# A two-layer DiT kernel on one core: the 1/rms of the q and k norm groups as a power on GpSimd, a copy moved to ScalarE, and the exponential's table loaded at another place

## The reference, cut to what matters

```python
def rmsnorm(x, g):
    xf = x.astype(jnp.float32)
    y = xf * lax.rsqrt(jnp.mean(xf * xf, axis=-1, keepdims=True) + EPS)
    return (y * g.astype(jnp.float32)).astype(x.dtype)
...
    q = (rmsnorm(q_lat, qc_g) @ w_q_up).reshape(b, n, MLA_HEADS, QK_DIM)
    kv = (rmsnorm(kv_lat, kvc_g) @ w_kv_up).reshape(b, n, MLA_HEADS, NOPE_DIM + V_DIM)
    q_nope = rmsnorm(q[..., :NOPE_DIM], qn_g)
    q_rope = rmsnorm(q[..., NOPE_DIM:], qr_g)
    k_nope = rmsnorm(kv[..., :NOPE_DIM], kn_g)
    ...
    q_rope = apply_axial_rope(q_rope, cos[:, None, :], sin[:, None, :])
    k_rope = apply_axial_rope(k_rope, cos, sin)
```

## Time and profile before

| | |
|---|---|
| median of three runs | 1451.29 us (1451.26 to 1451.75) |
| the profiled execution's own time | 1451.35 us |
| span in its trace | 1449.6 us |
| PE busy | 1416.5 us, 98% of the span |
| DVE busy | 996.3 us, 69% |
| ACT busy | 521.2 us, 36% |
| POOL busy | 86.7 us, 6% |
| mean granted TensorE clock | 0.995 of full |

### The profile page before, as it was taken

One profiled execution on the slowest core, in us unless ns is written; L12 is line 12 of the kernel. 1 busy time (PEld: TensorE's weight loads), 2 busy tenths in 40 slices (PEclk: granted clock), 3 DMA queues, 4 the chain that ended last, 5 costly groups with the idle time before them and its releaser, 6 DMA issues.

```text
span 1449.6 us, 20646 instructions
## 1 busy us (share of the span) xinstructions
PE 1416.5 (98%) x7940; PEld 1224.0 (84%) x7940; DVE 996.3 (69%) x1532; ACT 521.2 (36%) x841; POOL 86.7 (6%) x125
## 2 busy tenths in 40 slices
PE   6999899999999999999999999989999999999998
PEld 3788798889888888888888888878999888888887
DVE  5587887779866666666575678788667555555555
ACT  4352865243231122122221225476445323223322
POOL 0023700000000000000000000350000000000000
PEclk9999999999999999999999999999999999999999
DMA  9742012423543333324333412301032223322324
GB/s 389 296 131 88 1 45 73 146 88 119 184 146 117 94 122 117 121 81 158 116 100 102 144 45 64 111 15 56 4 103 91 98 90 100 99 87 89 112 91 142
DMA packets 42968, 158.62 MB, mean 109 GB/s; under 512 B 5152, under 2 KB 6560, under 8 KB 41760
## 3 DMA queue, kind: packets, MB, share of 16 engines
q1 hardware_dynamic: 42912, 157.87, 32.7%
HBM read 155.76 MB, written 2.10 MB: 109 GB/s over the span
## 4 chain that ended last, share of the span: by engine, by line
PE 84%; DVE 9%; ACT 3%; DMA 2%; issue 2%; SPq 0%; DVEq 0%; ACTq 0%
PE ps L734 68%; PE ps L653 4%; PE ps L655 4%; PE ps L654 4%; DVE w_lo L1428 1%; DMA ada_step<-in_w_step 1%; DVE tmp L1553 1%; DVE H_lo L1562 1%; PE ps L882 1%; PE ps L667 1%; DVE ss L1495 1%; DVE nmax L1771 1%; DMA w_raw<-in_w_main 1%; DVE pt_lo L1568 1%; ACT w_hi L1072 1%
## 5 line engine op out<-in xcount | busy, mean ns | idle before, releaser
L734 PE MATMUL ps<-H_hi,w_hi 128*128 128x512 f32 (+1 forms) x1280 | 448.8, 351 | 3.9 <-DVE H_lo L1562 2.6
L734 PE MATMUL ps<-H_lo,w_hi 128*128 128x512 f32 (+1 forms) x1280 | 447.4, 350 | 0.0
L734 PE MATMUL ps<-H_hi,w_lo 128*128 128x512 f32 (+1 forms) x1280 | 447.1, 349 | 0.0
L1072 ACT ACTIVATE w_hi<-w_raw 128x1024 fp32r<-128x1024 f32 x180 | 187.5, 1055 | 421.8 <-PE ps L734 368.8
L734 PEld LDWEIGHTS ps<-H_hi,w_hi 128*128 128x128 f32 x1280 | 242.3, 189 | 37.4 <-DVE H_lo L1562 3.8
L734 PEld LDWEIGHTS ps<-H_hi,w_lo 128*128 128x128 f32 x1280 | 242.2, 189 | 31.6
L734 PEld LDWEIGHTS ps<-H_lo,w_hi 128*128 128x128 f32 x1280 | 242.3, 189 | 30.8
L1575 DVE SCALAR_TENSOR_TENSOR X<-ps,mod,X 128x512 f32<-128x512 f32 (+1 forms) x296 | 181.1, 645 | 110.4 <-PE ps L734 88.1
L1428 DVE TENSOR_TENSOR w_lo<-w_raw,w_hi 128x1024 fp32r<-128x1024 f32 x180 | 221.7, 1242 | 37.3 <-ACT w_hi L1072 36.3
L734 PE MATMUL ps<-inner_hi,w_hi 128*128 128x512 f32 (+1 forms) x528 | 188.1, 356 | 0.3 <-DVE X L1575 0.3
L734 PE MATMUL ps<-inner_lo,w_hi 128*128 128x512 f32 (+1 forms) x528 | 187.5, 355 | 0.0
(11 more groups left out here) (210 smaller groups left out, 1836.7 us busy)
## 6 DMA issues: line engine op xcount, KB each, us to landing
w_raw<-in_w_main SPq DMA_DIRECT2D x182, 512.0 KB, 3.3
ada_raw<-in_w_ada SPq DMA_DIRECT2D x73, 512.0 KB, 4.1
ada_step<-in_w_step SPq DMA_DIRECT2D x7, 2048.0 KB, 16.7
X<-in_x SPq DMA_DIRECT2D x2, 1024.0 KB, 6.5
cb<-in_cvec SPq DMA_DIRECT2D x2, 1024.0 KB, 7.2
out_x<-X SPq DMA_DIRECT2D x8, 256.0 KB, 4.0
rtab<-in_rope SPq DMA_DIRECT2D x4, 384.0 KB, 9.2
X<-in_ctx SPq DMA_DIRECT2D x1, 1024.0 KB, 19.5
```

Of the source, the lines that this page charges most:

```text
L734: ins = pe.matmul(job.ps(a, b), ww[:, wsl], xx[:, xk, a:b], start=first and n == 0, stop=last and n == 2)
L1072: act.activation(w_hi[c % 4][:], w_raw[c % 2][:], ACT.Copy).then_inc(chunk_hi, 1)
```

## The change

It has five parts.

1. The root and the reciprocal of the 12 sums become one power with the exponent -0.5, on POOL: `inverse_root_q` (8 columns, both groups of q) and `inverse_root_k` (4 columns). ACT's `root_part` and DVE's `inverse` are gone. The mean's division is folded into the tables and gains (a factor of the root of 64 or 128).
2. DVE adds width times epsilon to the sums ahead of the power (`with_eps`), once for q and once for k.
3. Of the powers, those of tile 0 stand inside the rotation of the rotary key, and those of tile t+1 behind the addition of tile t, each in POOL's one stream.
4. The rounded copy of the rotated part goes from POOL to ACT (`rotated_hi`): that of tile t-1 stands between the square of k and the copy of v of tile t; in layer 0 that of tile 5 stands ahead of `turned_hi(5)`.
5. The one-column exponential goes from line 1334 to right behind the root of the latents, where from then on no root follows before the attention.

```diff
         pool.memset(lat_ss[:], 1.0).then_inc(consts, 1)
+        pool.memset(part_eps[:, 0:4], ROPE * EPS)
+        pool.memset(part_eps[:, 4:12], NOPE * EPS)
+        pool.memset(part_pow[:], -0.5)
...
-        def rotate(src, n, tab, done, before, scratch):
+        def rotate(src, n, tab, done, before, scratch, root_q, root_k):
...
             pool.tensor_tensor(a, src, rtab[:, tab, 0:n], ALU.mult).then_inc(done, 1)
+            root_q(0)
             for h in range(2):
...
             last.then_inc(done, 1)
+            root_k(0)
             pool.wait_ge(done, before + 2)
             pool.tensor_tensor(src, a, b, ALU.add).then_inc(done, 1)
...
+            def inverse_root_q(t):
+                pool.wait_ge(b_rt[L], parts(L, t, "q"))
+                pool.tensor_tensor(part_rms[:, t % 2, 0:8], part_sums[:, t % 2, 0:8], part_pow[:, 0:8], ALU.pow).then_inc(b_rc[L], 1)
+
+            def inverse_root_k(t):
+                pool.wait_ge(b_rt[L], parts(L, t, "k"))
+                pool.tensor_tensor(part_rms[:, t % 2, 8:12], part_sums[:, t % 2, 8:12], part_pow[:, 8:12], ALU.pow).then_inc(b_rc[L], 1)
...
                 pool.tensor_tensor(src, rgain[:], rope_b[:], ALU.add).then_inc(b_rot[L], 1)
-                pool.wait_ge(b_rot[L], 5 * t + 3)
+                if t + 1 < qtok(L):
+                    inverse_root_q(t + 1)
+                if t + 1 < TOK:
+                    inverse_root_k(t + 1)
+                pool.wait_ge(b_rot[L], 5 * t + 4)
                 hi, lo = (q_rs[L][t % 2][:, :, ROPE * n:ROPE * (n + 1)] for n in range(2))
-                pool.tensor_copy(hi.bitcast(F32R), src).then_inc(b_rot[L], 1)
-                pool.wait_ge(b_rot[L], 5 * t + 4)
                 pool.tensor_tensor(lo, src, hi, ALU.subtract).then_inc(b_rot[L], 1)
+            for t in range(qtok(L) + 1, TOK):
+                inverse_root_k(t)
...
             act.activation(lat_ss[:], lat_ss[:], ACT.Sqrt).then_inc(lat_rt[L], 1)
+            act.activation(warm[:, 0:1], ones[:, 0:1], ACT.Exp)
...
+            def rotated_hi(t):
+
+                act.wait_ge(b_rot[L], 5 * t + 3)
+                src = qn[t % 2][:, 0:ROPES].rearrange("p (h f) -> p h f", h=HEADS)
+                act.activation(q_rs[L][t % 2][:, :, 0:ROPE].bitcast(F32R), src, ACT.Copy).then_inc(b_rot[L], 1)
...
-                if t < qtok(L):
-                    root_part(t, "rope")
-                    root_part(t, "nope")
+                if 0 < t <= qtok(L):
+                    rotated_hi(t - 1)
...
-                root_part(t, "k")
...
-            act.activation(warm[:, 0:1], ones[:, 0:1], ACT.Exp)
+            if qtok(L) == TOK:
+                rotated_hi(TOK - 1)
             turned_hi(TOK - 1)
...
-            dve.tensor_scalar(qg[:, 0:1], V(L, V_QN), SCALE, None, ALU.mult).then_inc(tab_ok[L], 1)
+            dve.tensor_scalar(qg[:, 1:2], V(L, V_KN), NOPE ** 0.5, None, ALU.mult)
+            dve.tensor_scalar(qg[:, 0:1], V(L, V_QN), SCALE * NOPE ** 0.5, None, ALU.mult).then_inc(tab_ok[L], 1)
...
+            def with_eps(t, first, last):
+
+                cols = slice(4 * KINDS.index(first), 4 * KINDS.index(last) + 4)
+                dve.wait_ge(b_sum[L], sections(L, t, last))
+                dve.tensor_tensor(part_sums[:, t % 2, cols], part_sums[:, t % 2, cols], part_eps[:, cols],
+                                  ALU.add).then_inc(b_rt[L], 1)
...
                     sums(t, "nope", q_sq[L][:, ROPES:HEADS * HQ], NOPE)
+                    with_eps(t, "rope", "nope")
                 dve.wait_ge(b_sq[L], parts(L, t, "k"))
                 sums(t, "k", kn[m][:], NOPE)
+                with_eps(t, "k", "k")
                 if t < qtok(L):
-                    inverse(t, "rope", "nope")
+                    dve.wait_ge(b_rc[L], parts(L, t, "q"))
...
-                dve.wait_ge(b_sum[L], sections(L, t, "k"))
-                inverse(t, "k", "k")
+                dve.wait_ge(b_rc[L], parts(L, t, "k"))
```

More of the change, by code:

```diff
@@ L179, in build @@
     part_rms = sb("part_rms", [P, 2, 12])
+    part_eps = sb("part_eps", [P, 12])
+    part_pow = sb("part_pow", [P, 12])
     tok_rms = sb("tok_rms", [P, 8])
@@ L1267, in turned_hi @@
                 job.ready(act)
-                for kind, dst, o, scale in (("q", q, 0, qg[:, 0:1]), ("k", k, 512, V(L, V_KN))):
+                for kind, dst, o, scale in (("q", q, 0, qg[:, 0:1]), ("k", k, 512, qg[:, 1:2])):
                     if kind == "k" or t < qtok(L):
@@ L1645, in _ @@
                 gb = rgain[:, n:n + 1].to_broadcast([P, TOK, ROPE])
[L1646 removed]
+                dve.scalar_tensor_tensor(rtab[:, n], rtab[:, n], SCALE * ROPE ** 0.5 if n < 2 else 1.0, gb, ALU.mult,
                                          ALU.mult).then_inc(tab_ok[L], 1)
[L1648 removed]
+            dve.tensor_scalar(qg[:, 1:2], V(L, V_KN), NOPE ** 0.5, None, ALU.mult)
+            dve.tensor_scalar(qg[:, 0:1], V(L, V_QN), SCALE * NOPE ** 0.5, None, ALU.mult).then_inc(tab_ok[L], 1)
             ada = 0
@@ L1721, in sums @@
                                   ALU.add).then_inc(b_sum[L], 1)
-            def inverse(t, first, last):
-                x = part_rms[:, t % 2, 4 * KINDS.index(first):4 * KINDS.index(last) + 4]
-                dve.wait_ge(b_rt[L], sections(L, t, last))
-                dve.reciprocal(x, x).then_inc(b_rc[L], 1)
-                dve.wait_ge(b_rc[L], parts(L, t, "k" if last == "k" else "q"))
+            def with_eps(t, first, last):
[3 more added lines that the diff above has]
+                                  ALU.add).then_inc(b_rt[L], 1)
             def normed(t):
```

9 lines of the change are left out of this document (1 added, 8 removed).

## The result

The changed kernel took 1475.59 us at the median (1474.55 to 1476.0, 4 runs), the kernel before 1451.51 us beside it (1451.26 to 1451.75, 4 runs). The ratio is 1.0165 with a 95% interval of 1.0153 to 1.0178: 24.1 us slower. The forecast was 1458.2 us with a range up to 1470.0. It had the sign, the place and the queue at each front right, and the size wrong by 17.4 us; the time lies above the range. What carried most of the time, POOL as the engine that every tile waits for, was a rival with a chance of 0.25.

A forecast was written before the change was run, and what follows sets the result against it. It took the stage per tile, where four engines are nearly full, as the place that counts. Layer 0's 3.5, layer 1's 2.5 and the clock's 0.8 us, 6.8 on 1451.35, gave 1458.2 us; 8-in-10 range 1454 to 1470.

The forecast's parts named there:

- the queue at each front: POOL's instructions ahead of tile 1 delay DVE's multiplication of tile 1 by 2.9 us in layer 0, 2.7 in layer 1.
- X: Time of POOL's power over q's 8 columns, taken as 0.5 us, between 0.20 and 1.18.
- Y: Time of POOL's power over k's 4 columns, taken as 0.3 us, between 0.20 and 0.7.
- The upper row: POOL's longest two-input instruction of the same kind, 1.18 us, taken as upper end for the 8-column power.
- POOL becomes the bound: Rival: in the stage per tile POOL leads once both powers total 0.8 us; about 1468 us at upper ends; chance 0.25.
- a queue with a cheap power: The forecast's own case: POOL's queue delays the stage per tile; 1458.2 us, own range 1455.5 to 1461; chance 0.58.
- What was to be won back: On DVE, two additions replace two reciprocals: 0.22 us less for each tile behind the first, 0.9 us in layer 0.
- the end of layer 0: ACT's rounded copy of tile 5 waits for POOL's addition, reaching q at 175.4, not 171.90; layer 0 loses 3.5 us.
- The clock: Wider PE gaps at the end of the stage may lower the granted clock; counted at 0.8 us.
- slow first use: Rival: POOL's first power is longer once because its code is fetched; 1458.5 us with a few tenths; chance 0.05.
- the round trips and the table decide: Rival: tile 1's power comes in time, so the queue costs nothing; 3.0 us less, 1448.4 us; chance 0.04 for faster.
- The slack: DVE's 2.2 us idle in 32, most ahead of tile 0; chance 0.08 for enough to end within 0.2%.

The follow-up runs named there:

- the ladder: Kernel before plus products and powers of 1, 2, 4, 8, 16 columns on idle POOL, each twice; run once, 1451.75 us beside 1451.32.
- with products: Changed kernel with a product of the same shape in place of each power, order and waits unchanged; 1458.63 us.
- the copy on POOL and products: Changed kernel with a product in place of each power and the rounded copy back on POOL; 1454.69 us.

## Why the prediction was wrong in size

**The step that failed is the price of the power.** "I take X = 0.5 and Y = 0.3, near the lower row, because 8 columns are few" chose the wrong end, and both ends were too low. X was 1.65 us with an upper bound of 1.18, and Y 1.01 with one of 0.7. The reason given for the choice, few columns, was a guess that the ladder refutes: a power is paid by the column, at 0.16 us. The upper row was no bound at all, since it was the longest product, and a product's length can't bound another operation's. The prediction said that beyond the upper row "the time is open above", and ended its range there all the same.

**With the price, the sum comes out.** The prediction's own terms are 2X + Y at each front and, from X + Y = 0.8 on, X + Y - 0.8 for each of six further tiles. With 1.65 and 1.01 that is 2 x (2 x 1.15 + 0.71) = 6.0 us and 6 x 1.86 = 11.2 us, and 1458.2 + 17.2 = 1475.4 us, against 1475.6 measured. The rival "POOL becomes the bound" was what happened, since X + Y = 2.66 lies far behind its point of 0.8; the forecast's own case, a queue with a cheap power, had 0.58.

**But the sum's agreement is partly luck.** For short powers the sum gives 1456.8 us and 1458.6 was measured; for the length of the powers it gives 18.6 us and 16.8 was measured. The two errors of 1.8 us cancel. The second fits DVE's period, taken as 5.02 us: with products it was 5.25, so that a tile led by POOL (6.76 us at the full clock) is longer by 1.5 us and not by 1.86, in six tiles. And a term was missing. The same sum for the kernel with the power for k alone gives 1458.2 + 0.2 + 2.5 = 1460.9 us, and 1467.6 was measured. The prediction hadn't reckoned with the trip of k from DVE to POOL and back: k's inverse root is asked for 0.4 us after its sums are made. In the changed kernel that trip is covered in the tiles with q, since POOL leads there by its own work. In the two tiles of layer 1 without q it shows: DVE waits 1.61 and 1.12 us for the power, and from k to k these tiles take 5.01 and 4.52 us, where they took 3.84 and 3.85. These 1.8 us stand nowhere in the sum.

```profile
993.37 0.69 DVE L1768 TENSOR_TENSOR kn<-ps,part_rms 128x512 f32<-128x512 f32 x1 [1.61 <-POOL part_rms L632]
```

**The front, layer 0.** In the changed kernel the order was as laid out: first power at 142.95 (142.8 said), then 144.57, 145.87, 146.85 and tile 0 at 147.81, the addition at 150.43, the second power behind it at 151.11, DVE at 152.79. With products, DVE's multiplication of tile 1 stood 7.54 us behind the first sums (140.71 to 148.25), where it stood 5.52 before: 2.0 us late. The prediction's 2.9 less 0.7 for a short power is 2.2.

**What was to be won back** is hardly there. With the copy on POOL and products, tiles 2 to 5 lie 5.09 us apart (154.19 to 169.46), 0.15 us less than before; with the copy on ACT, 5.25, which is nothing. The 0.1 us for an addition of eps was too little, for the one over 8 columns took 0.47 us beside POOL's work.

**The copy on ACT** was held to be nearly free apart from the end of layer 0. It costs 3.7 us with short products. Two faults, too small a base here and the gain above, are why the kernel with products took 1458.6 and not the 1456.8 that the prediction's sum gives for 0.2 us each. Part of this is the clock: from `q_lo` of tile 5 to the first reduction the profiled execution with the copy on ACT has 4.00 us, at a granted clock of 0.50 (176.00 to 179.95), and the one with the copy on POOL 2.95, at 1.00 (173.00 to 176.86).

**The parts of the 24.1 us**, each as the difference of neighbours in the table: 3.6 us for the queue, the additions and the early table, 3.7 for the copy on ACT, 8.2 for the longer instruction for k and 8.6 for that for q. In the other order of adding them the powers are 8.6 for q and 8.2 for k, so these two add.

**The clock** was given 0.8 us. The granted clock was 0.88 in both stages, below the full 1.00 of before, while PE waited for 12.8 of 47 us in layer 0. In layer 0 rows show two places where the profiled execution paid for it. The projection of k and v for tile 3 ran at 0.50, the lower level of 1.2 GHz; POOL's power for k came later by that, and the tile took 7.13 us between neighbours of 6.74 and 6.76:

```profile
162.40:165.20 2.80, 2.76 (x7) 2.10 (x8) 2.67 (x5) 0.26 (x1) 2.62 (x6) 0.50 0.00 0
```

At the end 3.51 us pass from `q_lo` of tile 5 to the first reduction (186.76 to 190.27), at 0.62 from 187.00 on; before it was 2.95 us, at 1.00. Together that is 0.9 us, close to the 0.8. It isn't the same in each execution: the kernel with the table load late has 2.97 us at that end, and the two traces of the kernel with the copy on ACT alone have 2.95 and 4.01. The clock is so a small part of the 25.1 us of the stages.

**The other rivals.** No slow first use showed, neither in the ladder nor in the changed kernel, where the first power took 1.66 us and the others 1.65. (The Trainium skill, GPSIMD Engine Reference, section "Instruction dispatch", would have some 6 us ahead of a first call of freshly loaded code; no run here shows it for a power.) That the round trips and the table decide fell with the late table, which changed nothing; the kernel with the inverse root on ACT shows what DVE's reciprocals are worth when nothing is put in their place, 2.7 us; that the prediction had 3.0 for round trips and table is chance, for that kernel loads the exponential's table as before. The slack was read too kindly: of DVE's 2.2 us "most of it ahead of tile 0" is 0.93 us.

## What to carry to other kernels

An operation that the trace doesn't show must not be bounded by rows of a cheaper operation, however alike in shape: price it in a short ladder of widths, or leave the range open on that side. A small instruction that is moved to another engine must be held against two limits, that engine's work in a period, and the time between the making of its input and the use of its output. And where four engines are equally full, moving work between them has no price of its own: the same copy cost 8 us, 4 us or nothing that could be told, by which engine led.
